# The fourth mixing tile goes behind the transposes of the MLP rows, and the expert ring gets ten slots

## The reference

```python
def hierarchical_moe(xn, wg, bg, we, be, w_gate, w_up, w_down):
    ...                                   # group by softmax, top 2 of its 8 experts, two weights per token
    xs = xf[tok]                          # tokens ordered by expert
    h = jax.nn.silu(lax.ragged_dot(xs, w_gate, sizes)) * lax.ragged_dot(xs, w_up, sizes)
    y = lax.ragged_dot(h, w_down, sizes) * weights.reshape(-1)[order][:, None]
    out = jax.ops.segment_sum(y, tok, num_segments=T)
for layer in range(2):
    x = x + mixer(rms_norm(x, norm_mix[layer]))          # layer 0: attention and RG-LRU, layer 1: gMLP
    x = x + memory_cross_attention(rms_norm(x, norm_cross[layer]), rms_norm(mem, norm_mem[layer]), ...)
    x = x + hierarchical_moe(rms_norm(x, norm_ffn[layer]), ...)
```

## Time and profile before

| | |
|---|---|
| median of 3 runs (lowest, highest) | 1974.9 us (1973.99, 1977.34) |
| profiled execution, its own time | 1975.79 us |
| its span, first to last instruction | 1973.7 us |
| TensorE busy | 1887.8 us, 96% of the span |
| VectorE, ScalarE, GpSimd busy | 782.1, 543.7, 95.1 us |
| mean granted clock | 0.987 |
| read from HBM | 486.44 MB, 248 GB/s over the span |

### The profile page before, as it was taken

The page is one execution under the profiler, slowest core; times in us unless marked ns, Lnnn a source line. Parts: engine busy times, 40 slices in busy tenths (PEclk is TensorE's granted clock), DMA queues, the critical chain, the costliest instruction groups (busy, mean ns, idle before and its releaser), DMA issues.

```text
span 1973.7 us, 22387 instructions
## 1 busy us (share of the span) xinstructions
PE 1887.8 (96%) x9232; PEld 1208.9 (61%) x9232; DVE 782.1 (40%) x1176; ACT 543.7 (28%) x1008; POOL 95.1 (5%) x122
## 2 busy tenths in 40 slices
PE   7999999898999999999799999999899999999997
PEld 6875778676454544544588877777674444544543
DVE  4466564435232322322433346455361322322322
ACT  3426353533111111111244333445341111111110
POOL 2200010000000000000100022100000000000000
PEclk9999999999999999999899999999999999999999
DMA  6210342125999999999633312332128999999996
GB/s 237 86 64 22 109 148 86 44 90 206 403 417 413 414 416 407 420 414 414 239 104 127 110 51 80 128 107 86 46 86 355 417 419 412 416 414 410 418 413 286
DMA packets 95833, 490.05 MB, mean 248 GB/s; under 512 B 7761, under 2 KB 7825, under 8 KB 46449
## 3 DMA queue, kind: packets, MB, share of 16 engines
q1 hardware_dynamic: 92832, 478.18, 61.3%
q0 software_dynamic: 2320, 8.29, 1.2%
q10 hardware_dynamic: 576, 2.10, 0.3%
HBM read 486.44 MB, written 2.10 MB: 248 GB/s over the span
## 4 chain that ended last, share of the span: by engine, by line
PE 87%; DVE 5%; ACT 4%; issue 2%; DMA 1%; POOL 1%; SPq 0%; POOLq 0%; DVEq 0%; ACTq 0%
PE ps L635 24%; PE ps L1028 23%; PE ps L1043 11%; PE ps L993 6%; PE ps L632 6%; PE ps L1014 6%; PE ps L950 1%; ACT wh L518 1%; PE ps L831 1%; PE ps L931 1%; PE ps L673 1%; PE ps L1007 1%; DVE wl L527 1%; PE ps L1035 1%; DMA ring<-in_ab_w_in 1%
## 5 line engine op out<-in xcount | busy, mean ns | idle before, releaser
L1028 PE MATMUL ps<-ring,xg 128*64 128x512 f32 x1536 | 339.8, 594 | 0.3
L527 DVE TENSOR_TENSOR wl<-ring,wh 128x512 fp32r<-128x512 f32 x280 | 198.8, 720 | 331.2 <-ACT wh L518 330.0
L518 ACT ACTIVATE wh<-ring 128x512 fp32r<-128x512 f32 x280 | 174.1, 629 | 364.4 <-PE ps L635 287.4
L1028 PEld LDWEIGHTS ps<-ring,xg 128*64 128x64 f32 x1536 | 107.2, 137 | 211.2 <-issue 210.5
L635 PE MATMUL ps<-wh,ah 128*128 128x512 f32 x544 | 218.5, 402 | 10.6 <-DVE wl L527 5.3
L635 PE MATMUL ps<-wh,al 128*128 128x512 f32 x544 | 214.9, 395 | 0.0
L635 PE MATMUL ps<-wl,ah 128*128 128x512 f32 x544 | 214.6, 394 | 0.0
L2169 DVE SCALAR_TENSOR_TENSOR hh<-ps,wcol,sg 128x512 f32<-128x512 f32 x32 | 36.8, 1151 | 394.9 <-PE ps L1028 394.9
L2190 DVE TENSOR_TENSOR x<-ps,x 128x1024 f32<-128x1024 f32 x128 | 150.5, 1219 | 82.3 <-PE ps L1014 82.3
L1043 PE MATMUL ps<-ring,hT 128*64 128x512 f32 x768 | 171.9, 595 | 10.3 <-issue 8.0
L1582 ACT ACTIVATE xg<-ps,grow 128x256 f32<-128x256 f32 x128 | 53.6, 471 | 288.0 <-PE ps L993 266.8
(11 more groups left out here) (301 smaller groups left out, 2533.6 us busy)
## 6 DMA issues: line engine op xcount, KB each, us to landing
ring<-in_moe_w_gate SPq DMA_DIRECT2D x96, 1024.0 KB, 10.7
ring<-in_moe_w_up SPq DMA_DIRECT2D x96, 1024.0 KB, 8.7
ring<-in_moe_w_down SPq DMA_DIRECT2D x96, 1024.0 KB, 7.8
slot<-in_moe_w_up SPq DMA_DIRECT2D x32, 1024.0 KB, 9.0
slot<-in_moe_w_gate SPq DMA_DIRECT2D x32, 1024.0 KB, 11.4
slot<-in_moe_w_down SPq DMA_DIRECT2D x32, 1024.0 KB, 9.1
ring<-in_x_wkv SPq DMA_DIRECT2D x16, 1024.0 KB, 5.0
ring<-in_c_w_in SPq DMA_DIRECT2D x16, 1024.0 KB, 5.8
```

The costliest lines, as they stand in the source:

```text
L518: act.activation(wh[:, t % STAGE, :], ring[:, unit % RING, 512 * s:512 * (s + 1)], ACT.Copy).then_inc(wh_ready, 1)
L527: dve.tensor_tensor(wl[:, t % STAGE, :], ring[:, unit % RING, 512 * s:512 * (s + 1)], wh[:, t % STAGE, :].bitcast(F32), ALU.subtract).then ...
L1028: mm = pe.matmul(ps[p * SLOTS:(p + 1) * SLOTS, bank, :], xg[:, b % 2, k, r * P + p * SLOTS:r * P + (p + 1) * SLOTS], w(p)[:, k % 4, :], st ...
```

## The change

Three edits belong together. Mixing tile 3 of the pair before moves behind the transposes of `hh`. The down stage waits for three of the four additions (tiles 0, 1 and 2) of that pair. The expert ring gets two more slots, `slot8` over `gain` and `slot9` over `work`; their first loads wait until those buffers are free, and the load of layer 1's first gain moves from before the expert phase to after the last use of `slot8` in it.

```diff
-MOE_RING = 8
+MOE_RING = 10
@@ ring_plan
-            last.pop(RING, None)
-            last.pop(RING + 1, None)
+            for s in range(RING, MOE_RING):
+                last.pop(s, None)
@@ buffers
+        slot8 = sb("slot8", [P, UNIT], over="gain")
+        slot9 = sb("slot9", [P, UNIT], over="work")
@@ slot
-            mine = ring[:, s, :] if s < RING else (slot6, slot7)[s - RING][:, :]
+            mine = ring[:, s, :] if s < RING else (slot6, slot7, slot8, slot9)[s - RING][:, :]
@@ free_slot
                 elif SLOT[unit] == RING + 1:
                     sp.wait_ge(acc_done, PLAIN["ncross", l, TM - 1] + 1)
+                elif SLOT[unit] == RING + 2:
+                    sp.wait_ge(nat_ready, nats_upto("cross", l))
+                elif SLOT[unit] == RING + 3:
+                    sp.wait_ge(S["half_squares"], 2 * TM * (l + 1))
+                    sp.wait_ge(S["small_lo"], l + 2)
@@ do_down
-                        after(pe, S["y_added"], 4 * (q0 + q))
+                        after(pe, S["y_added"], 4 * (q0 + q) - 1)
@@ pair
                     if q:
                         do_mix(q - 1, 2, Y)
-                        do_mix(q - 1, 3, MIX)
                     pe.wait_ge(S["h_ready"], q0 + q + 1)
                     after(pe, S["hT_ready"], q0 + q)
                     hidden_T().then_inc(S["hT_done"], 1)
+                    if q:
+                        do_mix(q - 1, 3, MIX)
@@ gpsimd
                 if l + 1 < LAYERS:
-                    load_gain("mix", l + 1)
                     wait_taken(pool, ("route", l, 0))
                     ...
                                        pattern=[[0, C_GROUPS], [-1, P]], channel_multiplier=1).then_inc(S["ws_masked"], 1)
+                    u0 = PLAN["moe", l][0]
+                    last = max(u for u in range(u0, u0 + EXPERTS * 6) if SLOT[u] == RING + 2)
+                    pool.wait_ge(stage_used, STAGES * PAIRS * l + (last - u0) // 2 + 1)
+                    load_gain("mix", l + 1)
```

## The result

The changed kernel takes 1961.86 us (median of 5 runs, 1957.28 to 1964.77). The kernel before took 1973.99 beside it (5 runs, 1973.65 to 1977.34). The ratio is 0.9937, interval 0.9926 to 0.9948. The profiled execution took 1961.86 us, span 1959.7, against a span of 1973.7 before.

The account below looks back on a forecast made before the run. TensorE was taken to set the pace, transfers nearly full too, its down stages waiting for a fourth addition. Pairs 1 to 13 give 3.5 us, the last 1.0; 4.5 per layer, 9.0 in all: 1965.9 us, range 1962.5 to 1971.5.

Parts of the forecast that it names:

- the order's price: Tile 3's products start slowly behind the transposes of `hh`: charged 0.09 us per pair, bounds 0 and 0.18.
- The wait removed: Pairs 1 to 13: the down stage no longer waits for the fourth addition, worth 0.36 us per pair.
- The last two pairs: No gathers before tile 2 there: last pair gains 1.0 us, last but one nothing, between -0.3 and 0.3.
- Ten slots: Expert ring: eight slots would not do with faster TensorE; two more gain nothing themselves but keep the 4.5 us per layer.
- the 0.9 us of the last stage: Kernel before: layer 0's last stage lands at 946.6 and is used at 947.53, 0.9 us later.
- the sum's 1.4 us: Lead left in the changed kernel at 415 GB/s: last stage lands at 941.6, used at 943.0.
- Expert loads take some 5 us longer from issue to landing: Sign expected in the changed profile, with the rate at 417 GB/s or more.
- The rival of the binding loads: Transfers stay at 415 GB/s, pairs at 30.3 us: 1970.3 us, chance 0.12; extreme form 1974.9 us, 0.02 of it.
- the deeper queue: Rival: five stages outstanding instead of four slow transfers, pairs 31.45 us at 400 GB/s: 1993 us, chance 0.05.
- The gain and the seam: Later gain load lands about 952.5, 6 us before its use: cost 0, between 0 and 1.6 us.
- the terms' low end of 1962.9: Median if every term takes its favourable extreme, 6.0 us gained per layer.

Follow-up runs that it names:

- kernel two: The kernel before with only the down stage's wait changed to three additions, order and eight slots as before: 1960.8 us, ratio 0.9941.
- kernel three: The kernel before with only tile 3 moved behind the transposes, wait still for four additions, eight slots: 1981.31 us, ratio 1.0041.
- kernel five: The changed kernel with tile 3 back in front of the transposes; wait for three additions and ten slots kept: 1959.1 us, ratio 0.9942.
- kernel one: The changed kernel with eight slots and the gain's load as before; move and wait for three additions kept: 1960.77 us, ratio 0.9939.
- kernel seven: The changed kernel plus 14 products with unused results in TensorE's idle time at the layers' seam: 1957.5 us, ratio 0.9930.
- kernel eight: The changed kernel with tile 3 moved in each layer's last pair alone, plus 14 unused products at the seam: 1959.72 us, ratio 0.9947.
- kernel nine: The changed kernel once more, unchanged, on another chip: 1962.03 us, ratio 0.9948.
- kernel eleven: Repeat of the changed kernel with tile 3 moved in each layer's last pair alone, ten slots, wait for three: 1958.94 us, ratio 0.9933.

## Why the forecast was right in sign and too small

The wait that was removed was the right one. The term that was most mis-sized is the order's price, 0.09 us per pair in the sum and 0.03 measured, 1.7 us over both layers; another 1.2 us are in no term of the sum.

**The wait removed: right in kind, its size 0.38 instead of 0.36.** Kernels two and three show the cause from both sides: with three additions awaited the stall goes, with four awaited it moves along with the fourth addition. The name `hT` in the view of waits was indeed that of an engine long done. By kernel five the wait is worth 4.88 / 13 = 0.38 us per pair; 0.2 us per layer more than the term.

**The order's own price: the step that failed.** "I charge 0.32 - 0.23 = 0.09 us per pair" was three times too much: it is 0.03 by kernel five against the changed one, 0.8 us per layer less. The stated lower bound was the nearer one, the start-up "only takes the place of one that is there now": the weights' own slow start goes as tile 3's comes. I had read the price from a row in which transposes were followed by long products, and not what the transposes were followed by before.

**The last two pairs.** The last pair gave 0.87 for a forecast of 1.0. From `hh`'s start to the down stage the forecast had 943.07 - 940.50 = 2.57 us and the trace has 2.70: the transposes take 936.71 - 936.29 = 0.42 us in front of tile 3 and not 0.36, and tile 3 1.10 and not 1.01. The rows of the changed kernel:

```profile
935.11 1.13 DVE L2177 SCALAR_TENSOR_TENSOR hh<-ps,wcol,sg 128x512 f32<-128x512 f32 x1 [12.47 <-PE ps L1035]
...
936.29 0.66 PE L1042 MATMUL ps<-ident,hh 128*128 128x128 f32 x4
936.71 0.47 PE L1021 MATMUL ps<-yh,selT 128*128 128x512 f32 x1
...
937.81 1.08 PE L1050 MATMUL ps<-slot,hT 128*64 128x512 f32 x4
```

The pair before it gave 0.01 for a forecast of 0, by the mechanism forecast: the wait is worth 0.35, and waiting for `hh` in front of the transposes, with the move's own price, takes it back. What I did not see is that both halves can be had by moving tile 3 in the last pair alone.

**Ten slots: the second step that failed.** "If TensorE takes weights faster, the eight slots would not do" is refuted by kernel one and, but for one pause, by kernel two. I had let the rate of 415 GB/s stand while TensorE's pace rose; but 415 was TensorE's own demand, as the first part of the prediction says, and the transfers followed to 421. The landings show it: over 66 stages in the middle of layer 0 they come on average 5.07 us apart in the kernel before, 5.11 in kernel three with its longer pairs, and 5.00 in the changed kernel, about a sixth of the pair each time, while the median is 4.96 to 4.97 in all three. The kernels with longer pairs only have more late ones (over 5.2 us: 8, 12 and 4 of the 66). Nor was the 0.9 us of the last stage the least lead of the kernel before: the last up stage of layer 0 landed at 936.66 and was used at 936.85, 0.2 us later. A lead of 0.8 to 1.2 us is left with eight slots in kernel one, 0.4 in layer 1 of kernel two. In the changed kernel the last stages land 6.0 and 6.5 us before their use, so the sum's 1.4 us was too careful by the same error. What the ten slots buy is the room for a pause. In layer 1 of kernel five a stage of the last pair landed 5.85 us behind the one before, the least lead was 4.8 us, and nothing was lost; two slots fewer, 5 us, would have used it up by estimate.

"Expert loads take some 5 us longer from issue to landing" did not come: in the middle of the layers it is 10.4 and 10.2 us before, 11.4 and 10.7 after (medians of each stage's second load). The stage of room went into the lead instead; steady down stages had landed some 7 us before their use and now some 11. The rival of the binding loads is out, as TensorE waits for no load. That of the deeper queue is out for this ring, as single loads took up to 15.2 us and the rate did not fall, but the loads under way at one time hardly grew.

The Trainium skill, "DMA: Bandwidth & Descriptors", section "Bandwidth", has two ceilings, 358 GB/s of HBM for a core and 435 of the ports. The windows of the steady pairs say 420 and 421, 17 to 18% over the first and 3% under the second. With this one core at work the first did not bind; whether the second would have, no run shows.

**The gain and the seam: right.** The load is issued at 941.77, when stage 95's product has run, lands 4.0 us later and is used at 952.34:

```profile
941.77 0.61 POOL L2327 DMA_DIRECT2D gain<-in_norm_mix  x1 [464.37 <-PE ps L1050]
...
952.34 2.48 DVE L1702 SCALAR_TENSOR_TENSOR nat<-x,rnorm,gain 128x1024 f32<-128x1024 f32 x2
```

From the down stage of pair 15 to there it is 952.34 - 937.81 = 14.53 us, before 958.58 - 944.07 = 14.51.

**The sum and the range.** The steps make 10.9 us, where the forecast had 9.0. The distance from 1965.9 to 1961.86 is then: 0.9 because the kernel before was 1973.99 beside it and not 1974.9, 1.9 from the terms above, and 1.2 that no step of the program accounts for. Without that last part the median would be 1963.1, inside the range. The best account of it is the granted clock, which goes along with the time but which no run held fixed. Of the kernel before, executions with a mean granted clock of 0.988 took 1976.6 us (mean of 2), with 0.992 1970.0 (7); of the changed one 1964.2 with 0.988 (3) and 1959.5 with 0.992 (4). One thousandth goes with 1.2 to 1.6 us, and the profiled execution of before was at 0.987, the lowest of that kernel. Over the 42 timed runs of the kernel before the median is 1972.4, over the 10 of the changed one 1961.95. The difference, 10.5, is near the 10.9 of the steps; the 12.1 between the two medians that were compared first is not. The range took in the bounds of the terms, 6.0 us per layer, and they held; it did not take in that a median of a few runs can lie 1 to 2 us beside the middle, which should have been added below the terms' low end of 1962.9.

What stays open: why the half levels fall differently in executions of the same program, and whether they could be held off. In kernel seven's trace the first half level at the seam was missing, in kernel eight's it was there in spite of the same 14 products.

## What to carry to other kernels

Where the view of waits names a releaser, compare the end of every instruction that the wait could mean with the start of the waiter, in the timeline: here 0.11 against 0.51 us told the true one, and a kernel that changes only the number in the wait is the cheapest test of it. When an instruction is moved, read the start-up costs at the place that it leaves as well as at the place where it comes to stand, and move it only in those iterations in which it pays. A rate that transfers show while the engine sets the pace is a demand and no limit, and changes of the size of a few microseconds need the granted clock of each execution beside its time.

## What the runs showed of the hardware

- Expert stages of 2.1 MB land 4.96 to 4.97 us apart in the median, 422 GB/s, with eight slots and with ten, and whether a load takes 9 or 15 us. Now and then one comes 0.5 to 2.6 us late (gaps of 7.0 us in kernel two and 7.6 in kernel nine), more often where the pairs are longer. With eight slots one late landing cost 1.2 us in one trace and none cost anything in another; with six slots the transfers fell to 385 GB/s.
- At the seam between the layers, where TensorE had stood idle for 4.8 to 4.9 us, the granted clock was at half level for 13.7 us (before, and ten slots alone), for 3.4 + 3.4 (after) or for 3.4 (kernel eleven). With 14 products in the idle time, which left 1.7 and 2.2 us of it, it was at full level for the transposes in one trace (kernel seven) and at half in the other (kernel eight). Transposes start 0.213 us apart at the half level and 0.109 at the full one.
- A copy that ends 0.15 us before its reader starts costs nothing (kernel two), and the reader of a semaphore starts 0.10 to 0.11 us behind the instruction that sets it (kernel three).
